# Two transformer blocks on one core: the normed rows stay in one place in SBUF through both merges and the recurrent projection

## The chip, the cores and the metric

The kernel is written for a Trainium2 chip and runs on one of its cores. The metric is the device time of one execution in microseconds (us), as the median of several runs. PE is the matrix engine, PEld its weight load, DVE, ACT and POOL are the vector, scalar and GpSimd engines, and SP is the engine that mostly issues DMAs. SBUF is the on-chip memory of 128 partitions. The trace gives the clock that PE was granted as a share of 2.4 GHz: 1.00 is 2.4 GHz and 0.50 is 1.2 GHz.

## The reference, cut to what matters

Everything is float32, with 1024 tokens of width 1024. `h` is what this document calls the normed rows: each block computes it once and reads it in several projections.

```python
# first block
h = modulate(rms_norm(x, norm1_g), sh1, sc1)
q, k, v, g, hy_u, gate_ret, gate_hy = split(h @ w_in + b_in)
ret = retention_readout(o_lat, g)                      # 1024 x 1024
mixed = sigmoid(gate_ret) * (ret @ ret_w_o) + sigmoid(gate_hy) * (hyena @ hy_w_o)
x = x + gt1 * (mixed @ w_out);  x = x + gt2 * moe_ffn(modulate(rms_norm(x, norm2_g), sh2, sc2))
x = rms_norm(x, final_norm_g)
# second block
h = rms_norm_2(x, norm_mix_g)
z_mla, z_rwkv, z_gate = split(h @ w_in_2)
gates = sigmoid(z_gate + gate_b)
mixed = gates[0] * (o_mla @ w_br_mla) + gates[1] * (o_rwkv @ w_br_rwkv)
x = x + mixed @ w_out_2;  x = x + hier_moe(rms_norm_2(x, norm_ffn_g))
```

## The kernel before, in words

The program is a row of phases. Each phase is a block of instruction streams, one for each engine, and at its end all engines meet before the next phase begins; where `Mem.retire` stands between two phases, the semaphores used so far are cleared too and the engines meet once more. Inside a phase the engines wait for one another through semaphores. Matrices in SBUF lie transposed: `hT` has 8 tiles `[128, 1024]`, the feature on the partitions and the token along the row, 4 MB in all.

First block (`first`). `hyena` computes `hT`. Its projection phase `hin` (`phase_taps`) holds PE, and POOL meanwhile copies `hT` to DRAM (`S.hT`, four copies of 1 MB) and then clears `S.rows` in 27 copies, waiting for each copy before the next (L1827). `retention_branch` reads `hT` for q and k (`phase_qk`), v and g. `phase_ctx` before that has its weights in an SBUF tensor of its own. `phase_retention` works head by head; ACT stores the turned output of a head into `hT` (`retT`, L675), over the normed rows, which nobody in this branch needs any more. Its state store lies in the memory of `hyT`, the hyena output, which was saved to DRAM as `S.hyT`.

`phase_merge` ("merge1") computes `mixed`. For each of 8 output tiles (a loop of 4 with two weight slots, `s`) and each token half `h`, PE makes four accumulations in the order `turn = (2, 0, 1, 3)`: part 2 is the first branch (here `ret @ ret_w_o`, 8 matmuls), parts 0 and 1 are the two gates from the normed rows (8 matmuls each), part 3 is the second branch (here `hyena @ hy_w_o`, 4 matmuls). ACT takes the sigmoid of the gates, DVE multiplies and adds. SP loads the weights of a slot in the order parts 0, 1, 2, 3, all on one semaphore `full[s]`, and PE waits for all of them before the first matmul of the slot (L1244); before part 0 it also waits for `asided`. POOL issues the list `aside` through `copy_aside`: the first `needed` copies without waiting, and each later one only after the one before has landed. In merge1 the list begins with the four tiles of `S.hT` into a fresh `h2T`, then `S.hyT` into `hyT` (2 MB), and PE needs these five; then come four tiles of `x` into `K.X`.

Second block (`second`). `mla` fills a new `hT` and saves it to `S.hT`; the tensor is released after the attention. `rwkv` allocates one again and `phase_rwkv_consts` reloads it on SP as the last of nine loads, 4 MB in one copy; DVE waits for all nine, and at the end of the phase `phase_taps` ("taps") can begin. The tensor is released again and `phase_rwkv_chunks` uses the room for its chunk operands (`lev`, `arb`, `ark`, `rw`, `kv`). Then come `phase_rwkv_out` (mostly DVE), a `Mem.retire`, and merge2 with a third `hT`, again loaded by POOL (four copies, `needed` = 4). In merge2 part 2 is `o_mla @ w_br_mla` (4 matmuls, from `oT`). With `crossed=True` SP loads two more copies of 128 KB for it (L1237), the weights with the partition halves exchanged. Part 3 is the recurrent branch (4 matmuls). `moe` then has an SBUF tensor of its own for the expert weights `wu`.

## Time and profile before

| | us |
|---|---|
| median of 3 runs | 4761.65 (4757.93 to 4768.38) |
| the profiled execution, whole time | 4767.13 |
| the profiled execution, span of the instructions | 4765.3 |

The span is the time from the first to the last instruction in the trace; 1.8 us of the profiled execution lie outside it. The profiled execution is 5.5 us above the median of the three runs and inside their spread. PE is busy for 87% of the span; DVE (27%), ACT (21%) and POOL (10%) are far below. All times inside the program are counted from the start of the span.

### The profile page before, as it was taken

To read this page: it belongs to the slowest core of one execution; us is meant where nothing else is said; L and a number is where in the kernel's file an instruction comes from. 1 tells how busy PE (TensorE), PEld (TensorE's weight loads), DVE (VectorE), ACT (ScalarE), POOL (GpSimd) and SP (SyncE) were. 2 spreads that over 40 slices of the span, in tenths; PEclk is the share of its full clock that TensorE was granted. 3 is DMA by queue.
4 is the path that set the end of the run, shared out by engine and by line. 5 is a ranking of instruction groups with operands and counts; after the bars stand their busy time and mean duration, and the time that the engine had idled before them with its cause. 6 is when DMAs were issued, how large, how long until landed. Compare 5 with 4: busy or idle time off the path is not lost. (4 is left out here: it accounts for less than half of the span.)

```text
span 4765.3 us, 96365 instructions
## 1 busy us (share of the span) xinstructions
PE 4151.1 (87%) x41717; PEld 2692.9 (57%) x41717; DVE 1283.6 (27%) x2329; ACT 1023.2 (21%) x2418; POOL 469.3 (10%) x675
## 2 busy tenths in 40 slices
PE   7898587997799988999979896998999979997995
PEld 2343244886344447888865443448898844444774
DVE  2424212113000141000023654225655520112002
ACT  2200100003100011222223332014444410011333
POOL 1010000000000000000010000005454410000112
PEclk8899798997899988999989998999999989998998
DMA  6362121100411109999982001100000031112998
GB/s 217 120 188 67 71 68 57 36 18 0 135 31 46 43 38 368 392 398 395 398 302 74 7 5 62 35 18 3 4 4 4 3 114 34 46 52 98 388 388 319
DMA packets 247592, 601.15 MB, mean 126 GB/s; under 512 B 36408, under 2 KB 154087, under 8 KB 226504
## 3 DMA queue, kind: packets, MB, share of 16 engines
q1 hardware_dynamic: 202655, 454.52, 26.3%
q0 software_dynamic: 28704, 115.90, 7.2%
q10 hardware_dynamic: 16010, 27.46, 1.6%
q8 instruction: 176, 2.88, 0.3%
q14 instruction: 47, 0.39, 0.0%
HBM read 522.59 MB, written 75.24 MB: 125 GB/s over the span
## 5 line engine op out<-in xcount | busy, mean ns | idle before, releaser
L1649 PE MATMUL experts_bank<-experts_uT,ex_wu 128*64 128x96 f32 x13312 | 568.7, 247 | 52.8 <-PE experts_bank L1635 28.7
L1649 PEld LDWEIGHTS experts_bank<-experts_uT,ex_wu 128*64 128x64 f32 x13312 | 557.0, 138 | 84.2 <-issue 84.2
L1839 PE MATMUL taps_bank<-rwkvh_hT,taps_w 128*128 128x512 f32 x480 | 212.9, 602 | 32.4 <-DMA taps_w<-in_w_in 26.3
L1281 DVE TENSOR_TENSOR merge_pr<-merge_bank,merge_sg 128x512 f32<-128x512 f32 x64 | 44.2, 691 | 711.5 <-ACT merge_sg L1268 437.8
L1722 DVE TENSOR_TENSOR experts_hT<-experts_si,experts_bank 128x384 f32<-128x384 f32 (+1 forms) x68 | 31.3, 460 | 723.0 <-PE experts_bank L1649 723.0
L1254 PE MATMUL merge_bank<-b2m_hT,merge_w 128*128 128x512 f32 x512 | 222.3, 592 | 0.0
L1254 PE MATMUL merge_bank<-mix_h2T,merge_w 128*128 128x512 f32 x512 | 222.3, 592 | 0.0
L1635 PE MATMUL experts_bank<-mixed_T,experts_hT 128*32 128x256 f32 (+1 forms) x2592 | 193.9, 451 | 0.0
L1839 PE MATMUL hin_bank<-mix_hT,hin_w 128*128 128x512 f32 x384 | 169.9, 601 | 14.7 <-DMA hin_w<-in_w_in 9.1
L1839 PEld LDWEIGHTS taps_bank<-rwkvh_hT,taps_w 128*128 128x128 f32 x480 | 91.0, 192 | 154.4 <-issue 148.0
L2109 POOL TENSOR_TENSOR rc_lev<-rc_arb,rwkv_level 128x256 f32<-128x256 f32 x192 | 153.7, 833 | 160.0 <-DVE rc_arb L2462 159.9
L1254 PEld LDWEIGHTS merge_bank<-b2m_hT,merge_w 128*128 128x128 f32 x512 | 97.3, 190 | 122.5 <-issue 122.5
L1254 PEld LDWEIGHTS merge_bank<-mix_h2T,merge_w 128*128 128x128 f32 x512 | 97.3, 190 | 122.5 <-issue 122.2
L1268 ACT ACTIVATE merge_sg<-merge_bank,all_cols 128x512 f32<-128x512 f32 x64 | 44.0, 687 | 546.3 <-PE merge_bank L1254 546.2
L2478 DVE TENSOR_TENSOR rc_xy<-rc_xy,rc_bank 128x256 f32<-128x256 f32 x288 | 120.6, 421 | 122.9 <-PE rc_bank L2123 117.2
L1635 PEld LDWEIGHTS experts_bank<-mixed_T,experts_hT 128*32 128x32 f32 x2592 | 110.4, 110 | 69.6
L1677 ACT ACTIVATE experts_uT<-experts_bank,all_modrun 128x96 f32<-128x96 f32 x296 | 99.3, 439 | 212.6 <-PE experts_bank L1630 212.6
L1254 PE MATMUL merge_bank<-mix_hT,merge_w 128*128 128x512 f32 x256 | 115.9, 607 | 30.0 <-DMA merge_w<-in_hy_w_o 25.8
L1839 PEld LDWEIGHTS hin_bank<-mix_hT,hin_w 128*128 128x128 f32 x384 | 72.8, 192 | 111.3 <-issue 111.3
L332 PE MATMUL vproj_bank<-vproj_w,mix_hT 128*128 128x256 f32 x512 | 113.9, 385 | 23.2 <-DMA vproj_w<-in_w_in 21.8
L2860 PE MATMUL mh_sc<-mla_KTs,mh_QT 128*128 128x512 f32 x256 | 120.7, 594 | 5.1 <-ACT mla_KTs L2905 5.1
L512 PE MATMUL qk_bank<-mix_hT,qk_w 128*128 128x512 f32 x256 | 113.9, 604 | 9.2 <-DMA qk_w<-in_w_in 8.1
(504 smaller groups left out, 6558.9 us busy)
## 6 DMA issues: line engine op xcount, KB each, us to landing
ex_wu<-in_expert_w SPq DMA_DIRECT2D x72, 2048.0 KB
mixed_T<-in_expert_w SPq DMA_DIRECT2D x36, 2048.0 KB, 22.4
ex_wu<-in_w SPq DMA_DIRECT2D x64, 1024.0 KB
b2z_Z<-in_w SPq DMA_DIRECT2D x32, 1024.0 KB, 12.9
keep_rows<-mix_hyT POOLq DMA_DIRECT2D x27, 768.0 KB, 4.7
keep_rows<-experts_yo ACTq DMA_DIRECT2D x68, 288.0 KB
mix_hT<-in_ada_w POOLq DMA_DIRECT2D x8, 2048.0 KB
merge_w<-in_w_in SPq DMA_DIRECT2D x32, 512.0 KB, 5.1
```

Of the source, the lines that this page charges most:

```text
L332: last = pe.matmul(bk[t][:, 0:width], xT[:, k, tok0 + t * P:tok0 + (t + 1) * P], wt[:, s, k, :], start=(k == 0), stop=(k == kt - 1))
L512: last = pe.matmul(bk[2 * s + h][:, :], wt[:, s, k, :], xT[:, k, h * HALF:(h + 1) * HALF], start=(k == 0), stop=(k == KT - 1))
L1254: last = pe.matmul(bk[4 * h + j][:, :], w[:, s, k0 + k, :], x[:, k, hh], start=(k == 0), stop=(k == n - 1))
L1268: act.activation(sg[:, h, j, :], bk[4 * h + j][:, :], ACT.Sigmoid, bias=K.cols[:, bass.ds(i * 2 + (s + gate_col + 8 * j), 1)]).then_inc(si ...
L1281: dve.tensor_tensor(pr[:, h, j, :], bk[4 * h + 2 + j][:, :], sg[:, h, j, :], ALU.mult).then_inc(prod, 1)
L1635: return pe.matmul(bk[4 + 2 * s + j][32 * c:32 * c + 32, at:at + n], hT[:, k * BT + 32 * tokens:k * BT + 32 * tokens + 32], wd[:, s, k, c0 ...
L1649: last = pe.matmul(bk[2 + j][c:c + 64, h * BT:(h + 1) * BT], wu[:, s, j, k, h * P + c:h * P + c + 64], uT[:, s, k, :], start=(k == 0), sto ...
L1677: last = act.activation(uT[:, slot, k, :], bk[k // 4][:, k % 4 * BT:(k % 4 + 1) * BT], ACT.Identity, scale=scale(k), bias=shift(k) if shif ...
L1839: last = pe.matmul(bk[s * 2 + h][:, :], wt[:, s, k, :], xT[:, k, h * HALF:(h + 1) * HALF], start=(k == 0), stop=(k == KT - 1))
L2109: gp.tensor_tensor(lev[d][:, l, :, :], arb[d][:, :, 0, :], W.level[:, d, l:l + 1, :].to_broadcast([P, J, CH]), ALU.mult).then_inc(pos[d], 1)
L2478: dve.tensor_tensor(xy[d][:, x, :, :], xy[d][:, x, :, :], b2(bk[d][bank]), ALU.add).then_inc(dvs[d], 1)
L2860: last = pe.matmul(sc[g % 2][:, half(x)], QT[:, h % 2, u * P:(u + 1) * P], KTs[:, h // 2 % 2 * 2 + h % 2, half(x)], start=True, stop=True)
```

## The change

It does five things.

1. The normed rows are no longer overwritten in the first block: retention stores its output into `qk` (queries and keys of the head that is done), which `first` now allocates, and merge1 reads the gates from `hT` itself. `h2T`, the copy of `hT` to DRAM in `hin` and the four reloads in merge1 are gone.
2. In `second`, one `hT` lives through `mla`, `rwkv`, the merge and `moe`. The reload in `phase_rwkv_consts` is gone. The chunk operands are views of `hT`'s memory (`hole`), so `hT` is lost there and reloaded for merge2: by SP, four copies at the start of `phase_rwkv_out`, on a semaphore `again`. The `Mem.retire` between that phase and merge2 is gone.
3. Both merges load a slot's weights in the order in which PE uses them (`turn`), each part on a semaphore of its own, and PE waits for a part right before its first use (only for `h == 0`).
4. `asided` is awaited before part 3 in merge1, for one copy (`hyT`), which POOL now issues first. In merge2 part 0 waits for `again`. POOL waits for every single copy in both.
5. `phase_ctx` has two thirds of its weights in the memory of `qk`, and the second expert layer has `wu` in `hT`'s memory.

```diff
@@ phase_retention
-                        act.activation(retT[:, bass.ds(h * 2 + x, 1), y * HALF:(y + 1) * HALF].rearrange("p a n -> p (a n)"),
+                        act.activation(qk[:, bass.ds(h + 4 * x, 1), y * HALF:(y + 1) * HALF].rearrange("p a n -> p (a n)"),
@@ phase_merge
-        full = m.sems("full0", "full1")
+        full = [m.sems(*[f"full{s}_{j}" for j in range(4)]) for s in range(2)]
-        asided = copy_aside(m, b, aside, needed)
+        part, count, loaded = needed
+        asided = copy_aside(m, b, aside, count if loaded is None else 1)
...
-                    for k0, n, src, off in srcs:
-                        sp.dma_start(w[:, s, k0:k0 + n, :], src[:, :, bass.ds(i * 256 + (s * P + off), P)]).then_inc(full[s], 16)
-                    for c in (0, 64) if crossed else ():
-                        sp.dma_start(w[c:c + 64, s, nk:nk + ka, :], ...).then_inc(full[s], 16)
+                    for j in turn:
+                        k0, n, src, off = srcs[j]
+                        sp.dma_start(w[:, s, k0:k0 + n, :], src[:, :, bass.ds(i * 256 + (s * P + off), P)]).then_inc(full[s][j], 16)
+                        for c in (0, 64) if crossed and j == 2 else ():
+                            sp.dma_start(w[c:c + 64, s, nk:nk + ka, :], ...).then_inc(full[s][2], 16)
...
-                    pe.wait_ge(full[s], i * (64 + 32 * crossed) + (64 + 32 * crossed))
                     for h in range(2):
...
                         for j in turn:
-                            if j == 0:
-                                pe.wait_ge(asided, 16 * needed)
+                            if h == 0:
+                                each = 48 if crossed and j == 2 else 16
+                                pe.wait_ge(full[s][j], i * each + each)
+                            if j == part:
+                                pe.wait_ge(asided if loaded is None else loaded, 16 * count)
@@ phase_rwkv_chunks
-        lev = sb2("lev", [6, J, CH])
+        lev = two([6, J, CH])          # likewise arb, ark, rw, kv: views of hole
@@ phase_rwkv_out
+        @b.sync
+        def _(sp):
+            for dst, src, sem in ahead:
+                sp.dma_start(dst, src).then_inc(sem, 16)
@@ hyena
-                   aside=tiles_of(S.hT, hT) + clear)
+                   aside=clear)
@@ first
-        retT, h2T = hT, mm.sb("h2T", [P, KT, SEQ])
+        retT = lambda k: qk[:, 4 * (k % 2) + k // 2, :]
...
-                    (w_in[:, :, 4608:], h2T), PLACES["b_in"][0] + 36,
-                    tiles_of(h2T, S.hT) + ((hyT[:, :, :], S.hyT),) + tiles_of(K.X, ...) + ..., 5)
+                    (w_in[:, :, 4608:], hT), PLACES["b_in"][0] + 36,
+                    ((hyT[:, :, :], S.hyT),) + tiles_of(K.X, ...) + ..., (3, 1, None))
@@ rwkv
-        with Mem(nc, "rwkvh") as mh:
-            hT = mh.sb("hT", [P, KT, SEQ])
-            phase_rwkv_consts(nc, I, K, W, aside=((hT[:, :, :], S.hT),))
+        phase_rwkv_consts(nc, I, K, W, aside=())
@@ second
-        rwkv(nc, I, K, S, w_in, Z)
-        Mem.retire(nc)
+            rwkv(nc, I, K, S, w_in, Z, hT, tuple((dst, src, again) for dst, src in tiles_of(hT, S.hT)))
...
-                        tiles_of(hT, S.hT) + tiles_of(K.X, S.x....) + ..., 4, crossed=True)
+                        tiles_of(K.X, S.x....) + ..., (0, 4, again), crossed=True)
```

## Rows read from the trace of the kernel before

**Rows 1.** The page: busy time of each engine, share of the span, instructions.
```profile
PE 4151.1 (87%) x41717; PEld 2692.9 (57%) x41717; DVE 1283.6 (27%) x2329; ACT 1023.2 (21%) x2418; POOL 469.3 (10%) x675
```
**Rows 2.** Windows: start:end, us, PE, PEld, DVE, ACT, POOL busy, PE clock, DMA share, GB/s.
```profile
1245.00:1629.00 384.00, 379.40 (x881) 166.34 (x879) 32.07 (x47) 27.12 (x36) 3.28 (x4) 1.00 0.13 35
3196.00:3843.00 647.00, 597.78 (x15900) 562.44 (x15900) 370.80 (x793) 269.94 (x693) 300.84 (x404) 0.96 0.01 3
```
**Rows 3.** Timeline, start of merge1: start, us, engine, line, operation [idle before <- releaser].
```profile
1211.66 1.00 SPq L1235 DMA_DIRECT2D merge_w<-in_w_in  x2
1211.75 2.12 POOL L127 DMA_DIRECT2D mix_h2T<-keep_hT  x4 [73.54 <-POOLq L48]
1212.84 2.65 SPq L1235 DMA_DIRECT2D merge_w<-in_ret_w_o  x1
1235.10 9.97 PE L1254 MATMUL merge_bank<-mix_hT,merge_w 128*128 128x512 f32 x16 [25.81 <-DMA merge_w<-in_hy_w_o]
```
**Rows 4.** Timeline, the constants of the recurrent branch and the start of taps.
```profile
2969.84 0.87 DVE L1902 TENSOR_SCALAR rwkv_headrk<-rwkv_headones,all_cols 128x128 f32<-128x128 f32 x4 [18.24 <-DMA rwkvh_hT<-keep_hT]
2975.59 17.00 PE L1839 MATMUL taps_bank<-rwkvh_hT,taps_w 128*128 128x512 f32 x32 [26.33 <-DMA taps_w<-in_w_in]
```
**Rows 5.** Timeline, the last work of the recurrent output and the start of merge2.
```profile
3843.57 1.23 DVE L2524 TENSOR_TENSOR rwkv_Y<-rwkv_Y 128x1024 f32<-128x1024 f32 x1 [0.33 <-PEq L48]
3858.61 1.29 DVE L2539 TENSOR_TENSOR b2z_Z<-ro_t,ro_bank 128x512 f32<-128x512 f32 x2
3861.38 1.00 SPq L1235 DMA_DIRECT2D merge_w<-in_w_in  x2
3880.75 6.38 PE L1254 MATMUL merge_bank<-b2z_oT,merge_w 128*128 128x512 f32 x8 [25.08 <-DMA merge_w<-in_w_br_mla]
```
**Rows 6.** DMA issues from 1211.6 to 1212.5 and at 2971.3: size, us to landing.
```profile
merge_w<-in_w_in SPq DMA_DIRECT2D x1, 512.0 KB, 7.2
merge_w<-in_w_in SPq DMA_DIRECT2D x2, 512.0 KB, 13.6
taps_w<-in_w_in SPq DMA_DIRECT2D x1, 512.0 KB, 4.1
```
**Rows 7.** DMA queues (packets, MB, share): 1211.6:1214.2, 1226:1231, 1235:1239, 1231.3:1235; q0 is POOL's.
```profile
q1 hardware_dynamic: 691, 0.35, 48.3%
...
q0 software_dynamic: 119, 1.69, 80.0%
q1 hardware_dynamic: 505, 0.26, 17.2%
...
q1 hardware_dynamic: 798, 0.40, 37.2%
...
q1 hardware_dynamic: 2134, 1.07, 116.9%
```
**Rows 8.** Windows: the first matmuls after an idle PE, in merge1 and in `qk`.
```profile
1235.10:1241.00 5.90, 5.90 (x7) 2.49 (x8) 0.00 (x0) 0.00 (x0) 0.72 (x1) 0.51 1.10 344
659.50:664.00 4.50, 4.48 (x6) 1.91 (x7) 0.00 (x0) 0.00 (x0) 0.00 (x0) 0.50 0.28 65
```
**Rows 9.** DMA packets from 2955 to 2958, and from 2958.3 to 2970.
```profile
DMA packets 477, 1.05 MB, mean 352 GB/s; under 512 B 105, under 2 KB 108, under 8 KB 467
...
DMA packets 140, 3.78 MB, mean 323 GB/s; under 512 B 17, under 2 KB 17, under 8 KB 25
```
**Rows 10.** Timeline, the last work of retention and the last clear copy in `hin`.
```profile
1209.46 1.57 ACT L675 ACTIVATE mix_hT<-ret_bank 128x512 f32 x3 [1.09 <-PE ret_bank L619]
373.39 0.63 POOL L1827 DMA_DIRECT2D keep_rows<-mix_hyT  x1 [5.20 <-DMA keep_rows<-mix_hyT]
394.60 0.59 PE L1839 MATMUL hin_bank<-mix_hT,hin_w 128*128 128x512 f32 x1
```
**Rows 11.** Timeline of PE: merge1 from one token half's start on, and a turn of taps.
```profile
1262.07 7.03 PE L1254 MATMUL merge_bank<-mix_hT,merge_w 128*128 128x512 f32 x16
2992.88 1.55 PE L1839 MATMUL taps_bank<-rwkvh_hT,taps_w 128*128 128x512 f32 x3 [0.29 <-PE taps_bank L1839]
```

More of the change, by code:

```diff
@@ L412, in _, with phase_ctx @@
                     act.activation(tmp[:, d, :], pos[:, 2 + d, :], ACT.Exp, scale=c).then_inc(tt, 1)
-def phase_ctx(nc, I, K, R, hcT, w_in):
+def phase_ctx(nc, I, K, R, hcT, w_in, slab):
     with Mem(nc, "ctx") as m:
         kv = m.sb("kv", [P, 2, 1536])
-        w = m.sb("w", [P, 3, KT, HALF])
+        third = m.sb("w", [P, KT, HALF])
+        w = [slab[:, 4 * g:4 * g + 4, :].rearrange("p a (b n) -> p (a b) n", b=2) for g in range(2)] + [third[:, :, :]]
         kd = m.sb("kd", [P, 2, 2, HALF])
@@ L439, in _ @@
                     for k in range(KT):
-                        last = pe.matmul(bk[g * 2 + t][:, :], hcT[:, k, t * P:(t + 1) * P], w[:, g, k, :],
+                        last = pe.matmul(bk[g * 2 + t][:, :], hcT[:, k, t * P:(t + 1) * P], w[g][:, k, :],
                                          start=(k == 0), stop=(k == KT - 1))
@@ L1227, in phase_merge @@
         srcs = [(0, KT, wg, 0), (KT, KT, wg, D), (2 * KT, ka, wa, 0), (2 * KT + ka, kb, wb, 0)]
+        at = lambda x, k, cols: x(k)[:, cols] if callable(x) else x[:, k, cols]
         @b.sync
@@ L1250, in _ @@
                             k0, n, x = ((0, KT, hT), (KT, KT, hT), (nk if crossed and h else 2 * KT, ka, aT), (2 * KT + ka, kb, bT))[j]
-                            if j == 0:
-                                pe.wait_ge(asided, 16 * needed)
+                            if h == 0:
[3 more added lines that the diff above has]
+                                pe.wait_ge(asided if loaded is None else loaded, 16 * count)
                             for k in range(n):
-                                last = pe.matmul(bk[4 * h + j][:, :], w[:, s, k0 + k, :], x[:, k, hh], start=(k == 0), stop=(k == n - 1))
+                                last = pe.matmul(bk[4 * h + j][:, :], w[:, s, k0 + k, :], at(x, k, hh), start=(k == 0), stop=(k == n - 1))
                             last.then_inc(mm, 1)
@@ L1994, in shaped, with phase_rwkv_chunks, two @@
     return len(OUT_O) * q + OUT_O.index(name) + 1
-def phase_rwkv_chunks(nc, K, W, Z, kinv, Y, bv):
+def phase_rwkv_chunks(nc, K, W, Z, kinv, Y, bv, hole):
     with Mem(nc, "rc") as m:
         sb2 = lambda name, shape: [m.sb(f"{name}{d}", [P] + shape) for d in range(2)]
-        lev = sb2("lev", [6, J, CH])
-        arb = sb2("arb", [J, 3, CH])
-        ark = sb2("ark", [J, 2, CH])
-        rw = sb2("rw", [J, 2, CH])
-        kv = sb2("kv", [2, J, CH])
+        ends = [0]
+        def two(shape):
+            size = int(np.prod(shape))
+            ends.extend((ends[-1] + size, ends[-1] + 2 * size))
+            return [hole[:, end - size:end].rearrange("p (a b n) -> p a b n", a=shape[0], b=shape[1]) for end in ends[-2:]]
+        lev = two([6, J, CH])
+        arb = two([J, 3, CH])
+        ark = two([J, 2, CH])
+        rw = two([J, 2, CH])
+        kv = two([2, J, CH])
         xy = sb2("xy", [2, J, CH])
@@ L3032, in retention_branch @@
             phase_norm(nc, "ctxnorm", K.X, 2, hcT, lambda k: K.mod[:, 1, 0, k:k + 1], lambda k: K.mod[:, 1, 1, k:k + 1], K, src=I["ctx"][0])
-            phase_ctx(nc, I, K, R, hcT, w_in)
-        qk = m.sb("qk", [P, 8, SEQ]); v = m.sb("v", [P, 8, D]); g = K.X
+            phase_ctx(nc, I, K, R, hcT, w_in, qk[:, :, :])
+        v = m.sb("v", [P, 8, D]); g = K.X
         b0 = PLACES["b_in"][0]
@@ L3074, in hyena, with moe @@
         phase_inverse(nc, I, K, prod, xc, hyT)
-def moe(nc, tag, I, K, S, T, w_out, mixedT, spare, mix_gate, hidden, scale, shift, run_cols, names, gate=None, ahead=None):
+def moe(nc, tag, I, K, S, T, w_out, mixedT, wu, spare, mix_gate, hidden, scale, shift, run_cols, names, gate=None, ahead=None):
     rgw, rgb, rew, reb, w1, w3, w2 = names
@@ L3082, in moe @@
     with Mem(nc, f"ex{tag}") as mx:
-        T.wu = mx.sb("wu", [P, 2, 2, KT, hidden])
+        T.wu = mx.sb("wu", [P, 2, 2, KT, hidden]) if wu is None else wu.rearrange("p k (s n) -> p (k s) n", n=hidden).rearrange("p (s j k) n -> p s j k n", s=2, j=2)
         T.be = mx.sb("be", [1, MAXB], I32)
@@ L3101, in first @@
         Mem.retire(nc)
-        retention_branch(nc, I, K, S, w_in, hT, hyT[:, :, :])
-        retT, h2T = hT, mm.sb("h2T", [P, KT, SEQ])
+        qk = mm.sb("qk", [P, 8, SEQ])
+        retention_branch(nc, I, K, S, w_in, hT, qk, hyT[:, :, :])
+        retT = lambda k: qk[:, 4 * (k % 2) + k // 2, :]
         mw = Mem(nc, "mixed", side="right")
```

52 lines of the change are left out of this document (25 added, 27 removed).

## The prediction

> **What bounds the kernel now.** I read the page first. PE is busy 4151 us of 4765.3, every other engine at most a quarter [rows 1]. So the time can only shrink where PE stands idle or where it does work that goes away, and this change takes no matmul away. The table of windows comes next. Inside merge1 PE is busy 379.4 of 384 us at full clock, and the chunk stage of the recurrent branch is PE's too (597.8 of 647 us) [rows 2]. Work of DMA, DVE or POOL beside these stretches costs nothing as long as it ends in time. Then the timeline at the seams. Three starts stand out, each because PE waits for a DMA: merge1 (idle 25.8 us before 1235.1) [rows 3], taps (26.3 us before 2975.6) [rows 4] and merge2 (25.1 us before 3880.75) [rows 5]. These three are all that the change can win, some 77 us less what a phase start always costs.
>
> **Why these starts are long.** A 512 KB weight load alone lands 4.1 us after its issue. In merge1 the first one takes 7.2 us, the second 13.6 [rows 6]. SP's packets are 512 B. Alone, SP's queue moved 2134 of them from 1231.3 to 1235, 577 per us; beside POOL's load of `hyT` (119 packets, 1.69 MB, in 5 us, so 14 KB each) it moved 505, or 101 per us; beside POOL's loads of `K.X` 798 in 4 us, 200 per us. In the first 2.6 us of merge1, before POOL's stream came, it moved 691 [rows 7]. So SP's weights crawl as long as POOL has 6 MB of large packets on the way, and PE waits for all of them.
>
> **Merge1.** Removed: four loads of 1 MB. Part 2's weights (`ret_w_o`, 1024 packets) are now SP's first and PE waits for them alone. The load goes out at 1211.7. Before POOL's stream starts at 1214.2 some 600 packets pass (691 less what a slower issue costs: SP spent 2.65 us on this load but 1.0 on two of the gates' [rows 3]). The stream of `hyT` is 2.1 MB at 1.69 MB in 5 us = 340 GB/s, so 6 us, and beside it the other 424 packets need 424 / 101 = 4.2 us. That is 1218.4; with about 1 us for issue and completion PE starts at 1219.4, 7.7 us after the issue, close to the 7.2 of the row. Then the later parts must not be late. Eight matmuls at half clock (0.857 us each, 5.9 us for 7 in [rows 8]) take PE to 1226.3. The gates' first half is 1024 packets more; `hyT` ends at 1220.2 and POOL's next copy needs some 3 us from landing to streaming (the wait, 0.7 us of issue, 2.5 us as at the start), in which SP moves 577 per us: there by 1222.5. The second gate has 1024 packets, from there on mostly at 200 per us, by 1227 and needed at 1229.7; `hy_w_o` 512, by 1229.5, needed at 1233.1. `hyT` itself is needed at 1233.1 as well and there at 1221. So merge1 gains 1235.1 − 1219.4 = **15.7 us**. Bounds: 4.1 us after the issue as for a load alone gives 19.3; if `hyT` and all pieces came at the pace of the second load (6.4 us apart), the last part would be 2.5 us late: 13.2.
>
> A rule of the Trainium skill (DMA: Bandwidth & Descriptors, section Queues, rings and completion order) says that a DMA engine takes turns between the queues packet by packet. The trace has 505 SP packets beside 119 of POOL, so more than one for one. By the rule taken literally SP would move about 150 packets beside `hyT`, the rest after it, and merge1 would start at 1220.7: the sum would be 1.3 us smaller.
>
> **Taps.** Removed: the 4 MB reload. DVE resumes at 2969.84 [rows 4]; the last 3.78 MB of that phase moved from 2958.3 to 2970 in 140 packets, which are the reload's, and before 2958 nearly all packets (467 of 477) are the small ones of the constants [rows 9]. From the last packet to DVE's start takes about 1.4 us (traffic ended near 2968.4). So DVE goes on at 2958.3 + 1.4 = 2959.7: **10.2 us**. Lower bound 9 (constants slower at the end), upper 12.5 (landing 2.5 us after the last issue at 2954.9). What is late next is the first weight of taps, issued after the phase as before, 4.1 us; it stays.
>
> **Merge2.** Three things. First, the reload is moved to SP at the start of the recurrent output phase: work there starts at 3843.6 and ends at 3859.9 [rows 5], 4 MB took 11.5 us in [rows 9] and 14.9 from issue to DVE's start, so it lands by 3858.5. SP has nothing else to do there, POOL and the others wait for nothing of it, and PE needs it only at 3870. Cost 0; if the cover were gone, up to 15 us. Second, the barrier with the clearing of semaphores goes: 1.48 us lie between DVE's last end (3859.90) and SP's first issue (3861.38) here, 0.63 between ACT's last end (1211.03) and SP's issue at merge1, where no clearing is [rows 3, 5, 10]. Gain 0.8, so the phase starts at 3860.6. Third, the first part is 512 KB in three copies (256, 128, 128 KB), 1024 packets. SP needs some 2.4 us to issue them, so I let only 450 pass before POOL's `K.X` stream; 574 at 200 per us are 2.9 us: 2.6 + 2.9 + 0.6 = 6.1 us after the phase's start, 3866.7. Next: four matmuls at half clock, to 3870.1; the first gate, 1024 packets, mostly after the 4 us of that stream, by 3869; the second by 3871, needed at 3873.5 at the earliest; part 3 by 3874, needed at 3877. The gain is 3880.75 − 3866.7 = **14.0 us**. Bounds 11 (each piece later by 3 us) and 15.5.
>
> **At nothing.** In `hin` four POOL copies go. The clear copies follow each other and end near 378, 17 us before PE's last matmul at 394.6 [rows 10], so earlier is worth 0; the load of the first weights there competes with a POOL copy before and after. Retention stores the same tiles to another address: 0. Slots `h` and `h + 4` are those of the head that is done, and no wait is added. The views in `phase_ctx`, in the chunk phase and in `moe` change addresses only: 0 as a value, with both signs open, since the trace cannot show another placement. PE gets 3 more waits for each of 16 slots, 48. Where PE has two waits between halves it shows no idle time at all (16 matmuls in 7.03 us from 1262.07), while a turn of taps costs 0.29 [rows 11]: between 0 and 13.9 us; I take 0, as merge1 is the same loop. POOL's `K.X` copies start some 10 us earlier and are needed after the merge. The half-clock start stays in all three places, as PE is still idle over 10 us; it lasted 5.9 us after 26 us of idleness and 4.5 after 8 [rows 8], which may bring up to 0.7 us each.
>
> **The sum.** 15.7 + 10.2 + 14.0 = 39.9 us. Against the profiled execution: 4767.1 − 39.9 = 4727.2, against the median of three runs: 4761.65 − 39.9 = **4721.8 us**, which I give. The profiled execution is 5.5 above that median, within the runs' spread.
>
> **The rivals.**
> (a) Better starts, 0.14. The first parts come as if alone (merge1 3.3 us earlier, merge2 0.9) and the half-clock starts shrink by 0.7 each: 6.3 more, 4715.5. For it: POOL has far less to move. Against: its stream begins 2.5 us in, and 1024 packets need longer.
> (b) Starved pieces, 0.13. POOL's copies follow so closely that every 512 KB needs 6.4 us. Merge1 loses 2.5, merge2 1.7 at the start and 3.0 at each gate: 10.2 less, 4732. For it: the 13.6 us of the second load [rows 6]. Against: POOL now waits after each copy.
> (c) The waits of PE cost 0.29 each, 0.05: 4735.7.
> (d) The reload isn't there when merge2 asks, so the change doesn't do what it says, 0.03: PE stands before the gates. If it took the pace at which POOL's 6 MB came in merge1 (about 19 us) it would still be in time; it would have to be held back, at 6 us: 4728.
> (e) Slower, 0.03. The chunk operands lie in another place, and POOL, DVE, ACT and PE pass them on in a chain of short steps for 647 us. If each step were 6.2% longer (2.5 ns for each of 15900 matmuls) the gain would be gone; at 10% the time is 4786. Nothing in the trace speaks for it: sizes and strides are the same.
>
> **How the numbers follow.** The forecast has 0.60, (a) to (e) 0.38; 0.02 is left for a loss of the whole gain in some way I don't name. The range from 4708 to 4738 holds the forecast with its bounds (the upper ones together give 7.4 us more gain, 4714.4; the lower ones 6.7 less, 4728.5), (a) to (d), and some us for chips that differ like the runs shown. A measurement of this kernel can tell about 0.2%, 9.5 us, from no change; the forecast is four times that. Faster by more than 0.2%: 0.95 (all but (e) and the rest), within 0.2%: 0.02, slower: 0.03.
>
> **What would show it.** In the profile after, PE's first matmul of merge1 comes about 8 us after SP's first issue and reads `qk`, merge2's about 6 after, and DVE's L1902 work about 5 us after the last constant's issue. No copy into a second `hT` in merge1, reload traffic in the recurrent output. PE shows no new idle time inside the merges, and the chunk stage keeps its 647 us. I am wrong if PE stops at the second part of a slot, if those starts stay above 12 us, or if the chunk stage is longer.

## The result, and the profile after

| | before | after |
|---|---|---|
| median of the runs, us | 4763.78 (4757.93 to 4768.38, 4 runs) | 4722.11 (4721.01 to 4723.89, 4 runs) |
| span of the profiled execution, us | 4765.3 | 4719.2 |
| its own time, us | 4767.13 | 4721.01 |

The ratio of the times is 0.9915, with a 95% interval of 0.9901 to 0.9928: 41.7 us less, where 39.9 were forecast. In a later set of runs, `after_again` below, the same two kernels gave 4756.75 and 4714.46 (0.9910, 0.9894 to 0.9925), 42.3 us less. One of that set's five runs of the changed kernel took 5770.99 us, at a mean granted clock of 0.73 where the other four (4710.15 to 4714.89) had 0.942 to 0.944, and is left out of the ratio.

The page of after, against [rows 1]. PE has the same 41717 matmuls and is busy for 5 us less; the span is 46.1 us shorter. The DMA engines move 12.6 MB less than before (601.15 MB), three times the 4.19 MB of `hT`: the copy in `hin`, the reload in merge1 and the one in the constants' phase.

```profile
span 4719.2 us, 96353 instructions
...
PE 4146.1 (88%) x41717; PEld 2690.6 (57%) x41717; DVE 1284.3 (27%) x2329; ACT 1020.9 (22%) x2418; POOL 462.5 (10%) x663
...
DMA packets 246297, 588.57 MB, mean 125 GB/s; under 512 B 36264, under 2 KB 153944, under 8 KB 226361
```

Merge1's start, timeline of SP, POOL and PE (start, length, instruction, in brackets the idle time before it and what ended it), against [rows 3]:

```profile
1208.66 0.37 SPq L1239 DMA_DIRECT2D merge_w<-in_ret_w_o  x1
1209.22 2.36 SPq L1239 DMA_DIRECT2D merge_w<-in_w_in  x2
1211.68 5.80 SPq L1239 DMA_DIRECT2D merge_w<-in_hy_w_o  x1
...
1208.81 0.54 POOL L127 DMA_DIRECT2D mix_hyT<-keep_hyT  x1 [72.14 <-POOLq L48]
...
1215.09 9.01 PE L1260 MATMUL merge_bank<-mix_qk,merge_w 128*128 128x512 f32 x16 [8.75 <-DMA merge_w<-in_ret_w_o]
1223.93 13.90 PE L1260 MATMUL merge_bank<-mix_hT,merge_w 128*128 128x512 f32 x32
1237.66 3.60 PE L1260 MATMUL merge_bank<-mix_hyT,merge_w 128*128 128x512 f32 x8
```

PE starts 6.4 us after SP's first issue, on `qk`, and no later group has a bracket: gates and `hyena` find their data. One matmul of the code is two entries in the trace: part 2 has 8 matmuls for a token half, and the line says x16.

The constants and the start of taps, against [rows 4]. DVE resumes 4.4 us after the last constant's issue, and what it waited for is a constant (`gup`), no longer the 4 MB:

```profile
2932.56 0.33 SPq L1892 DMA_DIRECT2D rwkv_gup<-in_g_up  x1
2938.47 2.35 SPq L1825 DMA_DIRECT2D taps_w<-in_w_in  x3
...
2936.98 0.87 DVE L1908 TENSOR_SCALAR rwkv_headrk<-rwkv_headones,all_cols 128x128 f32<-128x128 f32 x4 [7.34 <-DMA rwkv_gup<-in_g_up]
```

The recurrent output and merge2's start, against [rows 5]: the reload (SP, L2537), DVE's last product of the output phase, then merge2.

```profile
3811.29 1.92 SPq L2537 DMA_DIRECT2D b2z_hT<-keep_hT  x4
3828.24 0.39 SPq L1239 DMA_DIRECT2D merge_w<-in_w_br_mla  x1
3828.83 1.46 SPq L1241 DMA_DIRECT2D merge_w<-in_w_br_mla  x2
...
3826.39 1.29 DVE L2558 TENSOR_TENSOR b2z_Z<-ro_t,ro_bank 128x512 f32<-128x512 f32 x2
...
3835.69 5.98 PE L1260 MATMUL merge_bank<-b2z_oT,merge_w 128*128 128x512 f32 x8 [12.26 <-DMA merge_w<-in_w_br_mla]
```

The next table cuts all profiled executions, those of the experiments included, at the same places, in us. "Start 1": from SP's first weight issue of merge1 to PE's first matmul (before: 1211.66 to 1235.10). "Merge1": from that issue to the first issue of the phase behind it. "Idle": PE's idle time ahead of taps. "Recurrent": from there to the first reduction of the output phase, with the chunk stage in it. "Start 2": from that reduction to merge2's first matmul. "Merge2": from the reduction to the first issue behind merge2. "Rest": from there to the span's end.

| kernel | start 1 | merge1 | idle | recurrent | start 2 | merge2 | rest |
|---|---|---|---|---|---|---|---|
| before | 23.44 | 419.76 | 26.33 | 869.23 | 35.93 | 376.71 | 543.77 |
| after | 6.43 | 401.85 | 15.43 | 869.87 | 23.10 | 363.98 | 542.63 |
| after_again | 9.13 | 404.42 | 15.13 | 863.52 | 23.55 | 364.03 | 540.43 |
| all_parts | 14.11 | 411.53 | 15.53 | 869.49 | 28.23 | 369.92 | 546.83 |
| parts_alone | 5.20 | 408.99 | 26.00 | 865.79 | 31.52 | 371.42 | 543.85 |
| retire_back | 9.41 | 405.99 | 14.88 | 870.17 | 25.55 | 366.64 | 545.93 |
| reload_pool | 6.23 | 402.70 | 15.14 | 867.30 | 32.15 | 373.30 | 542.63 |
| pool_later | 4.28 | 400.92 | 15.17 | 866.98 | 19.96 | 360.51 | 542.39 |
| weights_ahead | 6.99 | 402.14 | 14.96 | 870.51 | 21.75 | 363.20 | 545.35 |
| taps_ahead | 9.29 | 404.31 | 5.83 | 870.10 | 22.91 | 363.41 | 542.83 |
| ahead_both | 4.07 | 400.07 | 5.86 | 866.49 | 21.08 | 362.60 | 539.64 |
| slot_ahead | 6.20 | 401.79 | 15.11 | 866.37 | 15.87 | 357.09 | 540.35 |
| best | 4.10 | 400.77 | 5.84 | 869.64 | 15.62 | 356.59 | 543.88 |

From before to after: merge1 17.9, the way to taps 10.9, merge2 12.7. That is 41.5 of the 46.1 us between the two spans; the other 4.6 lie in stretches whose code is the same. "Rest" shows how much that can be: 539.6 to 546.8 us without an edit to its code. Ahead of merge1 its first issue comes between 1204.8 and 1214.5 in the thirteen executions. So a stage is read from its own stretch, never from two spans. The runs of the experiments fall into three sets, each with its own runs of the kernel before; a gain is best compared with the kernel before of the same set (medians 4764.84, 4761.29 and 4756.75).

### The profile page after: what moved, and what is told of

Read it like the earlier page. It is cut to its first block and busy times, and to the rows that moved or that the text cites. A ratio compares the mean times of both kernels' runs of the same rounds, so it can differ in the third digit from the quotient of the medians.

```text
span 4719.2 us, 96353 instructions
## 1 busy us (share of the span) xinstructions
PE 4146.1 (88%) x41717; PEld 2690.6 (57%) x41717; DVE 1284.3 (27%) x2329; ACT 1020.9 (22%) x2418; POOL 462.5 (10%) x663
## 5 line engine op out<-in xcount | busy, mean ns | idle before, releaser
L1655 PE MATMUL experts_bank<-experts_uT,ex_wu 128*64 128x96 f32 x9216 | 391.0, 247 | 25.7 <-PE experts_bank L1641 22.1
L1655 PEld LDWEIGHTS experts_bank<-experts_uT,ex_wu 128*64 128x64 f32 x9216 | 384.7, 138 | 42.5 <-issue 42.5
L1845 PE MATMUL taps_bank<-b2z_hT,taps_w 128*128 128x512 f32 x480 | 211.6, 599 | 21.6 <-DMA taps_w<-in_w_in 15.4
L1260 PE MATMUL merge_bank<-b2z_hT,merge_w 128*128 128x512 f32 x512 | 222.3, 592 | 0.0
L1260 PE MATMUL merge_bank<-mix_hT,merge_w 128*128 128x512 f32 x512 | 222.3, 592 | 0.0
L1655 PE MATMUL experts_bank<-experts_uT,b2z_hT 128*64 128x96 f32 x4096 | 177.8, 248 | 27.2 <-DMA b2z_hT<-in_w 19.4
L1655 PEld LDWEIGHTS experts_bank<-experts_uT,b2z_hT 128*64 128x64 f32 x4096 | 172.3, 138 | 41.9 <-issue 41.9
L2123 POOL TENSOR_TENSOR b2z_hT<-b2z_hT,rwkv_level 128x256 f32<-128x256 f32 x192 | 153.7, 832 | 161.8 <-DVE b2z_hT L2476 161.7
L1260 PEld LDWEIGHTS merge_bank<-mix_hT,merge_w 128*128 128x128 f32 x512 | 97.3, 190 | 122.5 <-issue 122.5
L1260 PE MATMUL merge_bank<-mix_qk,merge_w 128*128 128x512 f32 x256 | 115.0, 603 | 12.9 <-DMA merge_w<-in_ret_w_o 8.8
```

The costliest lines, as they stand in the source:

```text
L1260: last = pe.matmul(bk[4 * h + j][:, :], w[:, s, k0 + k, :], at(x, k, hh), start=(k == 0), stop=(k == n - 1))
L1655: last = pe.matmul(bk[2 + j][c:c + 64, h * BT:(h + 1) * BT], wu[:, s, j, k, h * P + c:h * P + c + 64], uT[:, s, k, :], start=(k == 0), sto ...
L1845: last = pe.matmul(bk[s * 2 + h][:, :], wt[:, s, k, :], xT[:, k, h * HALF:(h + 1) * HALF], start=(k == 0), stop=(k == KT - 1))
L2123: gp.tensor_tensor(lev[d][:, l, :, :], arb[d][:, :, 0, :], W.level[:, d, l:l + 1, :].to_broadcast([P, J, CH]), ALU.mult).then_inc(pos[d], 1)
```

## The experiments

The theory: the gain is three shorter waits of PE for its first operands. The rivals: only the order of the loads or only the missing traffic brings it; the early reload or the new places cost something elsewhere.

### How much the order and the semaphores bring

`all_parts`: the changed kernel, all four parts waited for first.

```diff
                 for s in range(2):
+                    for j in turn:
+                        each = 48 if crossed and j == 2 else 16
+                        pe.wait_ge(full[s][j], i * each + each)
                     for h in range(2):
...
-                            if h == 0:
-                                each = 48 if crossed and j == 2 else 16
-                                pe.wait_ge(full[s][j], i * each + each)
```

> The changed kernel, but PE waits for all four parts of a slot's weights before its first matmul of the slot; the order of the loads and all placements stay. Theory (one part's weights are there soon, the other three need some 8 us more): merge1 starts at 13 to 16 us after SP's first issue instead of 6.4, merge2 at 13 to 16 instead of 7.45, and the gates find everything there; 12 to 18 us slower than the changed kernel, some 4737. Rival (the removed traffic of POOL alone brings the gain, the finer semaphores nothing): starts within 2 us of those of the changed kernel, under 4 us slower. Taps unchanged in both.

Measured: 4735.40 us (4731.79 to 4739.82), ratio to before 0.9935 (0.9918 to 0.9951): 29.4 us under the kernel before of its set, where the changed kernel has 41.7 and 42.3 in its own two, so 12.3 to 12.9 us of the gain are gone.

```profile
1221.19 9.52 PE L1260 MATMUL merge_bank<-mix_qk,merge_w 128*128 128x512 f32 x16 [16.47 <-DMA merge_w<-in_hy_w_o]
...
3847.68 5.27 PE L1260 MATMUL merge_bank<-b2z_oT,merge_w 128*128 128x512 f32 x8 [17.35 <-DMA merge_w<-in_w_br_rwkv]
```

The bracket now names the last part of the slot. The starts are 14.1 and 12.5 us after SP's first issue, in place of 6.4 and 7.5; merge1 is 9.7 us longer and merge2 5.9. The theory holds, though merge2 starts just before the 13 us that it gave as the earliest. The rival falls: less traffic alone does not bring the whole. It does bring the larger part: by the three stretches this kernel is still 25.8 us faster than before.

`parts_alone`: the kernel before, with order and semaphores only (the diff's lines of `phase_merge` from `full = ...` to the PE wait, and nothing else).

> The kernel before, with nothing but the order of the weight loads and one semaphore for each part in the merges; both reloads of hT stay on POOL. Theory (POOL's 6 MB hold both the gates' rows and the weights): PE starts some 8 us after SP's first issue, but then stands before part 0 until the rows are there, 15 to 20 us after the issue; 3 to 9 us faster than before in all, some 4757. Rival (the order is what counts): over 20 us faster, under 4743. Taps unchanged in both.

Measured: 4746.42 us (4742.99 to 4751.76), 0.9958 (0.9943 to 0.9972): 18.4 us faster than before, between what the two had expected.

```profile
1217.26 7.90 PE L1257 MATMUL merge_bank<-mix_hT,merge_w 128*128 128x512 f32 x12 [7.53 <-DMA merge_w<-in_ret_w_o]
1232.73 15.59 PE L1257 MATMUL merge_bank<-mix_h2T,merge_w 128*128 128x512 f32 x32 [5.84 <-DMA merge_w<-in_w_in]
...
3857.45 5.35 PE L1257 MATMUL merge_bank<-b2z_oT,merge_w 128*128 128x512 f32 x8 [20.62 <-DMA merge_w<-in_w_br_mla]
```

In merge1 the one 512 KB load slips through before POOL's stream is up (5.2 us), and PE then stands 5.8 us before the gates, 20.7 us after the issue. The theory had PE wait there for the rows. By the trace it is the first gate's weights that come last: the four tiles of `h2T` have landed by 1226.8, `hyT`, which this wait still includes, at 1232.0, the weights at 1232.7. They are SP's small packets behind POOL's 6 MB. And I had counted only the shorter wait and forgotten that part 2's matmuls are then already done: merge1 is 10.8 us shorter. In merge2 the first part is three copies and doesn't slip through: 14.9 us from SP's issue at 3842.52; the stretch is 5.3 us shorter. So of the 41.5 us that the change gains in the three stretches, 16 come with the order and the semaphores alone, which need no memory, and the other 25 need the rows in place. Order and separate waits without room bring 16, room without separate waits (`all_parts`, which keeps the order of the loads) about 26; together 41.5.

### The reload and the barrier

`reload_pool`: the four copies of `hT` go back to POOL at merge2's start.

```diff
-            rwkv(nc, I, K, S, w_in, Z, hT, tuple((dst, src, again) for dst, src in tiles_of(hT, S.hT)))
+            rwkv(nc, I, K, S, w_in, Z, hT, ())
...
-                        tiles_of(K.X, S.x.rearrange("(t p) d -> p t d", p=P))
+                        tiles_of(hT, S.hT) + tiles_of(K.X, S.x.rearrange("(t p) d -> p t d", p=P))
...
-                        + ((K.ffnrun[:, :], I["norm_ffn_g_2"].rearrange("l (p k) -> p (l k)", p=P)),), (0, 4, again), crossed=True)
+                        + ((K.ffnrun[:, :], I["norm_ffn_g_2"].rearrange("l (p k) -> p (l k)", p=P)),), (0, 4, None), crossed=True)
```

> The changed kernel, but the four copies that bring hT back are POOL's at the start of merge2, as before the change, not SP's during the recurrent output. Theory (the early reload is hidden where it is, and needed): PE starts merge2 with its own part as early as in the changed kernel or up to 3 us later, then stands before the gates until hT is there, 15 to 19 us after the phase's start: 5 to 10 us slower than the changed kernel, some 4729. Rival (what counts is only that part 2 does not wait): within 2 us. Rival (the reload costs its neighbours in the recurrent output as much): that phase gets shorter by over 1 us here.

Measured: 4732.08 us (4723.87 to 4734.32), 0.9925 (0.9908 to 0.9943): 32.8 under the kernel before of its set, 8.9 to 9.5 less than the changed kernel's gain, and merge2 is 9.3 us longer than in after. The size is right, the picture is not:

```profile
3829.07 0.37 SPq L1239 DMA_DIRECT2D merge_w<-in_w_br_mla  x1
...
3845.82 6.30 PE L1260 MATMUL merge_bank<-b2z_oT,merge_w 128*128 128x512 f32 x8 [21.55 <-DMA merge_w<-in_w_br_mla]
3851.96 13.90 PE L1260 MATMUL merge_bank<-b2z_hT,merge_w 128*128 128x512 f32 x32
```

PE does not start early and then stand before the gates; its own first weights need 16.7 us beside POOL's 4 MB, and once they are there the rows are, too. Traffic that nobody waits for yet delays the transfer that is waited for. The reload beside the output phase costs that phase next to nothing: from its first reduction to the start of its last two products DVE needs 13.80 us in after (3812.59 to 3826.39), 13.79 in before, 13.54 here. Its packets end there too. The packets of after from 3811.3 to 3828.2, and from 3823.0 on:

```profile
DMA packets 577, 4.20 MB, mean 249 GB/s; under 512 B 64, under 2 KB 64, under 8 KB 64
...
DMA packets 5, 0.02 MB, mean 3 GB/s; under 512 B 3, under 2 KB 3, under 8 KB 3
```

The 4 MB are through at 3823, some 12 us after the issue and 5 before merge2's first issue.

`retire_back`: the changed kernel with `Mem.retire(nc)` put back between the recurrent branch and merge2.

> The changed kernel with the barrier and the clearing of semaphores put back between the recurrent branch and merge2. Theory: SP's first issue of merge2 comes 0.8 to 0.9 us later after DVE's last end, and all else stays: 0.9 us slower, which only the profile can show. Rival (the barrier makes every engine and queue start together, or drains the reload): over 3 us later, or nothing at all.

Measured: 4725.65 us (4718.34 to 4731.69), 0.9910 (0.9893 to 0.9928), which can't be told from the changed kernel, as expected. SP's first issue comes at 3834.05, 1.60 us after DVE's last end (3831.17 + 1.28); in after it is 0.56. The barrier with the clearing costs 1.0 us, as [rows 5, 10] had it (0.8). Here "start 2" is 2.4 us longer than in after; the other 1.4 are those by which the weights landed later (8.8 us after the issue in place of 7.5), a spread the next runs show too.

### What sets the starts that are left

`after_again`: the changed kernel once more.

> The changed kernel once more, unchanged. If the 2 us by which its chunk stage was longer than before's, and the 3 us between its start of merge1 (6.4 us after the issue) and that of one relative (9.4), come from the run and not from the code, both can fall elsewhere here: the start within 6.2 to 9.4, the stretch from taps' second turn to the first reduction of the recurrent output within 850 to 855 us. If the code sets them, they are 6.4 and 853.9 again, within 0.3. Median 4722 within 5.

Measured: 4714.46 us, 42.3 below before on this chip. The same code starts merge1 9.1 us after the issue in place of 6.4, and its recurrent stretch is 863.5 us in place of 869.9. Both come from the run, not from the code. The spread is wider than I expected: from taps' second turn on the stretch is 847.5 us (2961.16 to 3808.64), outside the 850 to 855, and the median is 7.5 below 4722. Over the seven executions with the same start of merge1 (after, after_again, retire_back, reload_pool, weights_ahead, taps_ahead, slot_ahead) it takes 6.2 to 7.0 us four times and 9.1 to 9.4 three times, 7.7 in the mean.

`pool_later`: POOL waits, before its first copy in either merge, for part 2's weights.

```diff
     def _(gp):
+        gp.wait_ge(*held)
         for n, (dst, src) in enumerate(pairs):
...
-        asided = copy_aside(m, b, aside, count if loaded is None else 1)
+        asided = copy_aside(m, b, aside, count if loaded is None else 1, (full[0][2], 48 if crossed else 16))
```

> The changed kernel, but in both merges POOL issues its first copy only when part 2's weights of the first slot have landed. Theory (what remains of the start beyond a lone load's 4.1 us is POOL's large packets beside SP's): merge1 starts 4.5 to 5.5 us after SP's first issue in place of 6.4 (6.2 to 9.4 in the runs so far with the same start), merge2 5 to 6.5 in place of 7.45, and nothing is late afterwards: 2 to 5 us faster than the changed kernel, some 4719. Rival (SP's own issue and the three queued loads behind set the start): no start moves by over 0.5 us. Rival (the copies are late then): PE idle before hyT's part or DVE's rows in the phase after; 4 us slower or more.

Measured: 4713.07 us (4711.43 to 4714.69), 0.9899 (0.9882 to 0.9915); the changed kernel's ratios are 0.9915 and 0.9910. It is 48.2 us under its kernel before, 5.9 to 6.5 more than the changed kernel; the intervals overlap, so the reading goes by the stretches. Merge2 is 3.5 us shorter than in the changed kernel, merge1 0.9 to 5.1 shorter than in the executions with its start.

```profile
1209.45 0.37 SPq L1241 DMA_DIRECT2D merge_w<-in_ret_w_o  x1
...
1213.98 0.54 POOL L129 DMA_DIRECT2D mix_hyT<-keep_hyT  x1 [76.53 <-DMA merge_w<-in_ret_w_o]
...
1213.73 10.07 PE L1262 MATMUL merge_bank<-mix_qk,merge_w 128*128 128x512 f32 x16 [6.61 <-DMA merge_w<-in_ret_w_o]
...
3826.76 5.72 PE L1262 MATMUL merge_bank<-b2z_oT,merge_w 128*128 128x512 f32 x8 [9.23 <-DMA merge_w<-in_w_br_mla]
```

4.3 us in merge1 (also in `ahead_both` and `best`: 4.1) and 4.4 in merge2, from SP's issue at 3822.34: what a load alone takes, and earlier than the 4.5 and 5 us expected at the least. POOL's stream is the whole remainder, and its two values are gone with it. `hyT`, issued 4.4 us later than before, is still in time; PE has no bracket after its first. What the queues moved shows how POOL's stream does it. After, 1208.66 to 1211.17, 1211.17 to 1213.67 and 1213.67 to 1216.17 (one line of the first, two of the others), then `retire_back` from 1214.22 to 1216.72 and from 1216.72 to 1219.22 (2.5 and 5.0 us after its issue), then all of `pool_later` from 1209.45 to 1213.73 (queue, packets, MB, share; q0 is POOL's, q1 SP's):

```profile
q1 hardware_dynamic: 594, 0.30, 40.6%
...
q0 software_dynamic: 48, 0.79, 77.7%
q1 hardware_dynamic: 424, 0.22, 30.7%
...
q0 software_dynamic: 64, 1.05, 98.3%
q1 hardware_dynamic: 63, 0.03, 3.7%
...
q0 software_dynamic: 51, 0.84, 81.3%
q1 hardware_dynamic: 391, 0.20, 26.5%
...
q0 software_dynamic: 62, 1.02, 95.8%
q1 hardware_dynamic: 62, 0.03, 4.2%
...
q1 hardware_dynamic: 1675, 0.85, 74.9%
```

Once `hyT`'s stream is up, the two queues move the same number of packets: 63 beside 64, 62 beside 62, in the kernel before 102 beside 101 (1226 to 1230). POOL's have 16 KB, SP's 512 B, so SP's queue falls from over 570 packets per us to 25. The 424 beside 48 are a window that begins before the stream: in half-microsecond windows SP's queue passes 331 and 68 packets up to 1212.2, then 14, 13 and 5 beside 14, 13 and 5 of POOL's. In merge2, beside POOL's 4 KB packets of `K.X`, it is worse than one for one: SP's queue moves 6 beside 235 in after from 3830.74 to 3833.24, and then, from the end of that copy on, over 500 per us.

PE's part has 1024 packets. The 1024th of SP's queue moves 5.1 us after the issue in after, 4.4 to 5.1 in the four early executions, 8.0 in each of the three late ones and 3.1 to 3.2 in the three where POOL waits; PE starts 1.3 to 2.0, 1.2 to 1.4 and 0.9 to 1.1 us behind it. So the count of packets does say when this load lands. The two values differ in how many were through when POOL's tenth packet moved: 930 to 982 in the early executions, 871 to 897 in the late ones. The 42 to 94 that are missing then move within 1.3 to 2.0 us beside the stream. The 127 to 153 need nearly all of it: 126 to 131 of POOL's 144 packets are through before the last of them. Why fewer had passed by then in three executions stays open.

### Loads ahead of their phase

`weights_ahead`: the weights of merge2's first two slots are SP's in the recurrent output phase, slot 0, then `hT`, then slot 1. The buffer needs 28 KB of each partition (two slots of 28 tiles of 128 float32); `y2` and `t` of the output phase move to tiles 4 and 5 of `Z`, which nobody reads any more.

```diff
+            def early(sp):
+                w, full = got[0]
+                for s in range(2):
+                    for j in (2, 0, 1, 3):
+                        merge_load(sp, w, full, parts, w_in[:, :, 2592:], s, j, s * P, True)
+                    for dst, src in tiles_of(hT, S.hT) if s == 0 else ():
+                        sp.dma_start(dst, src).then_inc(again, 16)
```

> The changed kernel with merge2's weights of both first slots loaded by SP already in the recurrent output phase (first slot, then hT's four copies, then second slot); two tiles of that phase lie in dead rows of Z to make room. Theory (merge2's start is the landing of its first weights and nothing else): PE starts within 1.5 us of the phase's start in place of 7.45, 5.5 to 7 us less in merge2, some 4716. Rival (hT is late): the same start, but PE idle before the gates. Rival (DMA traffic slows the recurrent output): its 13.8 us from the first reduction to the last product grow by over 1 us.

Measured: 4719.71 us (4710.69 to 4725.51), 0.9905 (0.9888 to 0.9922): 41.6 under its kernel before, so nothing is gained on the changed kernel. No expectation had the reason:

```profile
3821.62 4.19 SPq L1225 DMA_DIRECT2D m2w_w<-in_w_br_mla  x2
3825.86 7.41 SPq L1223 DMA_DIRECT2D m2w_w<-in_w_in  x2
3833.31 2.70 SPq L1223 DMA_DIRECT2D m2w_w<-in_w_br_rwkv  x1
...
3828.86 1.28 DVE L2573 TENSOR_TENSOR b2z_Z<-b2z_Z,ro_bank 128x512 f32<-128x512 f32 x2
...
3836.90 3.78 PE L1276 MATMUL merge_bank<-b2z_oT,m2w_w 128*128 128x512 f32 x4 [10.98 <-DVEq L1295]
```

An issue that takes 0.4 us on an idle queue takes 2 to 4 here, with many 512-byte packets queued ahead of it. SP issued until 3836.0, 5.9 us after DVE's last end, and the phase ends when the last engine is through, SP too. PE's bracket names no DMA: the weights were there. Merge2 is only 0.8 us shorter than in after.

`slot_ahead`: the same with slot 0 alone; slot 1 is loaded at merge2's start.

> The changed kernel with only the first slot's weights of merge2 (and then hT) loaded by SP in the recurrent output phase; the second slot's loads stay in merge2. Theory (with both slots SP's queue was full, its last issues took 7.4 and 2.7 us, and the barrier at the phase's end waited for SP until 6.8 us after DVE's last product): SP is done before DVE, merge2's PE starts 0.8 to 1.5 us after DVE's last end in place of 8.0, and 6 to 7.5 us are gained on the changed kernel, some 4715. Rival (hT lands too late behind the weights): PE starts as early, but stands before the gates. Rival (something else holds the phase): no gain.

Measured: 4706.38 us (4704.28 to 4716.78), 0.9903 (0.9888 to 0.9919); 8.1 below `after_again` by the medians on the same chip, while the ratios' intervals overlap.

```profile
3808.43 2.30 SPq L3212 DMA_DIRECT2D b2z_hT<-keep_hT  x4
3820.44 0.38 SPq L1223 DMA_DIRECT2D m2w_w<-in_w_br_mla  x1
...
3820.93 6.39 PE L1278 MATMUL merge_bank<-b2z_oT,m2w_w 128*128 128x512 f32 x8 [4.97 <-DVEq L1297]
```

SP is done at 3810.7, and PE starts 0.75 us after DVE's last end (3820.18): merge2 is 6.9 us shorter than in both executions of the changed kernel. The theory holds, and beside `weights_ahead` it shows that slot 1's loads on SP's queue cost the gain there.

`taps_ahead`: the constants' phase loads taps' first three weight tiles; the constants are POOL's in taps, and `headrk` is made in the gates' phase.

> The changed kernel, but the constants' phase only loads the first three weight tiles of taps and does DVE's small work; POOL loads the constants during taps, and headrk is made in the gates' phase. Theory (after the change the way to taps is eight constant loads in a row, then one weight load, and neither needs the other): PE starts taps 5 to 6.5 us after SP's first issue of the constants' phase in place of 13.7, and no later stage grows by over 1 us: 6 to 8.5 us faster than the changed kernel, some 4715. Rival (the stretch is set by the barriers and code around the phases): still over 10 us.

Measured: 4711.61 us (4710.93 to 4713.13), 0.9895 (0.9879 to 0.9912): 49.7 under its kernel before, 7.4 to 8.0 more than the changed kernel.

```profile
2929.53 2.21 SPq L1890 DMA_DIRECT2D tapsw_w<-in_w_in  x3
...
2933.66 16.59 PE L1846 MATMUL taps_bank<-b2z_hT,tapsw_w 128*128 128x512 f32 x31 [5.83 <-DMA tapsw_w<-in_w_in]
```

PE starts 4.1 us after the issue, before the 5 us expected at the least; its idle time falls from 15.4 to 5.8, and no later stretch grows beyond what the same code shows elsewhere in the table.

`ahead_both` is `taps_ahead`, `weights_ahead` and, in merge1 only, POOL's wait.

> All three: taps' and merge2's weights ahead, and in merge1 POOL's first copy after part 2's weights. Theory (the stages are apart, so the gains add): 13 to 18 us faster than the changed kernel, some 4706. Rival (a saving in one stage is lost in the next): under 10.

Measured: 4706.87 us (4704.12 to 4708.02), 0.9886 (0.9869 to 0.9902): 54.4 under its kernel before, 12.1 to 12.7 more than the changed kernel's gain and so just under the 13 expected at the least; "start 2" has the full queue of `weights_ahead` in it. `best` has `slot_ahead` in its place.

> Taps' weights ahead, merge2's first slot ahead, and in merge1 POOL's first copy after part 2's weights. Theory (three stages apart, the gains add): 8.5 + 6.5 + 3 = 18 us faster than the changed kernel, some 4704, and faster than every other kernel here. Rival (a saving in one stage is lost in the next): under 12 us.

Measured: 4702.21 us (4700.89 to 4704.85), 0.9889 (0.9874 to 0.9904): 54.5 us under before and 12.3 under `after_again` on the same chip. That is less than the 18 expected and just above the rival's 12, and against the kernel before it is no faster than `ahead_both` (54.4), though it was expected to be the fastest. By stretches it is as the theory has it: 3.7 in merge1, 9.3 before taps, 7.4 in merge2 against `after_again`, 20.4 together. The spans differ by only 13.5. The recurrent stretch is 6.1 us longer (869.6 against 863.5), the rest 3.5, and between merge1 and the idle time before taps 1.3; ahead of merge1 it is 4.0 shorter. Some 1.3 in the recurrent stretch are taps' start at half clock (below); all else lies within what those stretches span for the same code, so the runs don't show that a saving is lost there, nor exclude a few us.

## Why the prediction was right, point by point

- **Merge1, forecast 15.7.** By the start 17.0 in the pair (23.44 to 6.43), 15.8 over the seven like executions. That their mean, 7.7 us after the issue, is the forecast to the tenth is luck: they lie at 6.2 to 7.0 and at 9.1 to 9.4, none between. The way of counting was right; two of its terms were off and partly cancelled. 600 packets before 2.5 us were right (594), but POOL's first packet moves only at 3.1 us, and by its tenth 967 were through, so 57 were left in place of 424. And beside `hyT` SP's queue moves some 29 packets per us and not 101: the window of [rows 7] from 1226 to 1231 is 102 beside 101 of POOL's up to 1230 and then 403 beside 18, when `hyT` was nearly through. From the 1024th packet to PE were 1.3 us, 1 was taken. Nor is SP's first issue slow (0.37 us, not 2.65).
- **The later parts**, in time as forecast, had more room than the prediction gave them. It took 8 matmuls of 0.857 us, 6.9 us, for the first part of a token half. But 8 matmuls are 16 entries of the trace: 9.97 us in [rows 3], 9.01 in after, and 6.9 us for each gate behind it. So the first gate is needed 2 to 3 us later than it said, the second 5 to 6, `hyT` 9 to 10.
- **Taps, forecast 10.2.** 10.9 (26.33 to 15.43); 10.8 to 11.5 with the others. DVE resumes 4.4 us after the last constant's issue; about 5 were forecast. `parts_alone`, where the reload is, has 26.00.
- **Merge2, forecast 14.0.** 12.8. The barrier: 0.8 forecast, 0.9 in the pair, 1.0 in `retire_back`. The reload hidden: shown. The mis-sized term is the first part beside POOL's `K.X`: 6.1 us after the issue forecast, 7.5 measured (7.2 to 8.8 in the four executions with this start). The 1024th packet of SP's queue was forecast at 5.5 us and moves at 5.9, but not by the pace of 200 per us: it nearly stands for 2.5 us and then runs. And PE starts 1.5 us after it, where 0.6 were taken.
- **At nothing.** 48 more waits: none shows, PE's groups follow each other in the merges. The places: the chunk operands now lie in `hT`'s slab, and the recurrent stretch is 863.5 to 870.5 us with them in eleven executions, 865.8 and 869.2 without in two. Rival (e) at its price of 40 us and more is refuted; a cost under some 3 us is not excluded. "Cover gone, up to 15 us" for the reload: `reload_pool` lost 9.3 in merge2.
- **The half-clock start, up to 0.7 us each for less idle time, taken as 0.** In the pair the first group after each of the three starts is shorter: 9.97 to 9.01 us in merge1, 17.00 to 15.63 in taps, 6.38 to 5.98 in merge2. But with the same start merge1's takes 8.54 to 10.18 in the other executions, and the length doesn't follow the idle time. Windows of PE at taps' start, the first and the second 3 us (after; then `taps_ahead`; then `parts_alone`), columns PE's busy time with its matmuls, granted clock as a share of 2.4 GHz, DMA share, GB/s:

```profile
2942.72:2945.72 3.00, 3.00 (x4) 0.50 1.01 251
2945.72:2948.72 3.00, 3.00 (x7) 0.95 0.00 0
...
2933.66:2936.66 3.00, 3.00 (x4) 0.50 1.15 291
2936.66:2939.66 3.00, 3.00 (x4) 0.50 0.10 26
...
2960.14:2963.14 3.00, 3.00 (x4) 0.51 1.06 261
2963.14:2966.14 3.00, 3.00 (x8) 1.00 0.00 0
```

At 1.2 GHz PE stayed for over 6 us where it had been idle for only 5.8 (`taps_ahead`), and for about 3 where it had been idle for 26 (`parts_alone`); before, idle as long, had over 6 (granted clock 0.50, 0.50, then 0.99). So taps' first turn takes 15.7 to 17.3 us, and less idle time doesn't make it shorter. Rival (a) lost its second half by this; its first half, a start as if alone, is what `pool_later` gives.
- **Rival (b)**, pieces 6.4 us apart, did not come: no part is late. Its loss in merge1 rests on the 8 matmuls above: with 9 and then 6.9 us for a part, pieces 6.4 us apart would have been in time. **(c)** and **(d)** are refuted above.
- **The rule on turns** between the queues. The pace of 101 per us that the sum took is refuted: beside `hyT` SP's queue moves as many packets as POOL's. The prediction had set 505 packets beside 119 against one for one; that window mixes, as said. Taken literally, one for one had merge1 start at 1220.7 (9.0 us after the issue), the sum 1.3 us smaller. The Trainium skill (DMA: Bandwidth & Descriptors, section Queues, rings and completion order) says that an engine takes turns between its queues packet by packet, and merge1's trace agrees, with 63 beside 64 and 62 beside 62; merge2's does not at first, with 6 beside 235, and why is open. The three late executions of merge1 start about where one for one had it (9.1 to 9.4), because the end of the load had to wait for nearly all of `hyT`. The pair's and three others start at 6.2 to 7.0 at the same pace, because 930 to 982 packets had passed before the stream, not 600.

The sum: 17.0 + 10.9 + 12.8 = 40.7 in the pair, 15.8 + 11.2 + 12.4 to 12.8 over the repeats, about 39.6, against 39.9 forecast; by the medians 41.7 and 42.3. The terms are off by +1.3, +0.7 and -1.2 in the pair, so the sum is closer than its parts. The medians' 2 us more than the stages stand in the spread of the unchanged stretches and are not explained further.

## What to carry to other kernels

An engine that waits for its first operand waits for the traffic around it, too. Order the loads by use with a semaphore for each, and hold a bulk copy back until the first small load is in: here that was free and brought the first load down to what it takes alone, 4.3 us. Beside a bulk copy the small load crawls: here its queue moved 512 B for every 16 KB of POOL's, or next to nothing. A load is best hidden in the phase before, if its issues are few enough that the issuing engine is done before the phase is: a full queue makes the issue itself slow, and the barrier waits for it.

Judge a stage by its own stretch over several executions of the same code. Here unchanged stretches differ by up to 7 us from execution to execution, and moving one load or one wait gains 3.5 to 9.6 in its stretch.

## What was not expected of the hardware

- Merge1's start has two values for the same code, 6.2 to 7.0 and 9.1 to 9.4 us, and one, 4.1 to 4.3, when POOL's copy waits. They go with how many of the 1024 packets pass before POOL's stream is up (930 to 982, or 871 to 897).
- SP's issue of a load takes 0.4 us on an idle queue, 5.80 behind three loads of 512 KB in packets of 512 B (merge1 in after), 7.41 for two in `weights_ahead`.
- Beside POOL's packets of 16 KB SP's queue of 512 B packets moves one for one, 25 to 30 per us in place of over 570. At the start of `K.X` in merge2, with packets of 4 KB, it moves 4 to 44 in 2.5 us.
- PE starts 0.9 to 2.0 us after the 1024th packet of its load in merge1. Where POOL waits, SP's queue has moved 1586 to 1675 packets by then, where it doesn't and the start is early, 1060 to 1075.
- The half-clock start lasts about 3 to over 6 us, without regard to whether PE was idle for 6 or 26 us.
